# Seven residual stages in split float32: the way up of the feed-forward by feature from the third block on, both parts of x in one 512-column product

## The chip, the core and the metric

The kernel runs on one core of one Trainium2 chip. Its engines are TensorE (PE in the profile; its weight loads are PEld), VectorE (DVE), ScalarE (ACT), GpSimd (POOL) and SyncE (SP), which here issues all DMAs. The metric is the device time of one execution in microseconds; less is better. It includes reading all weights from memory.

## The reference

One sequence of 256 tokens with 1024 features goes through seven residual stages: feed-forward, mLSTM mixer, feed-forward, feed-forward, Mamba-2 mixer, feed-forward, and a hybrid of attention and gated convolution with a final norm. The change touches the four feed-forward stages:

```python
D_FF = ((8 * D_MODEL // 3 + 127) // 128) * 128        # 2816
def swiglu(h, w1, w3, w2):
    return (jax.nn.silu(h @ w1) * (h @ w3)) @ w2

def sublayer(x, fn, g_pre, g_post, shift, scale, gate, weight):
    hmod = rms_norm(x, g_pre) * (1 + scale[:, None, :]) + shift[:, None, :]
    y = rms_norm(fn(hmod), g_post)
    return x + weight * gate[:, None, :] * y
```

Shift, scale and gate of every stage are products of a vector c with a large matrix (the modulation). All data are float32.

## The kernel before

**Arithmetic.** Every large product is made in float32r from split operands: a value is rounded to a high part, and the remainder is the low part. `three` (L1022) issues high x high, high x low and low x high, three matmuls, into the same PSUM region. `xhi` and `xlo` hold the parts of x: features 0 to 1023 in tiles 0 to 7, the gated products of the feed-forward in tiles 8 to 15, always as [feature, token].

**Units.** The weights come in units of 1 MB (128 x 2048). SP loads a unit to a ring of NS = 5 places (`load`, a place is free when its old unit is used), ScalarE rounds it (`hi`, L553), VectorE forms the remainder (`lo`, L1646; in quarters `lo_part`, L1651), and then TensorE may use it (`ready`). `w_in`, `w_hi`, `w_lo` and `w_used` count these steps, each in the order of the units, and every engine has its own place for them in a hand-written order. VectorE also takes two modulation units (`ada`, L1656) per block while they last, nine blocks' worth in a stage (six in the last).

**A feed-forward stage.** The 2816 hidden features are eleven blocks (NF) of 256. The way up of a block takes two units: half 0 has the first 512 input features, half 1 the others, and a unit holds 256 columns of w1 (gate) beside 256 of w3 (up). The way down of a block takes one unit. `first_two` makes blocks 0 and 1 into banks 4 to 7. From the third block on (i = 2 to 10) TensorE runs: the way up by token (`by_token`: x is the stationary operand, the weights are moved, 512 columns; token tile 0 to bank 4, tile 1 to bank 5), and then the way down of block i - 2 (`down`, for two token tiles, into banks 0 to 3, y).

By token the result is [token, feature], and the way down wants [feature, token]. ScalarE takes silu of the gate half (`silu`, L713), VectorE multiplies by the up half (`gate_up`, L1855), TensorE turns the product by four transposes into bank 6 (`turn`, L1238), ScalarE rounds it into `xhi` (`gated_hi`, L717), VectorE forms the remainder into `xlo` (`gated_lo`, L1861). The turn of block i - 1 stands in the middle of block i's way up:

```python
by_token(a, 0, 1, 5).then_inc(w_used, 1)
if i > 2:
    turn(i - 1)
by_token(a + 1, 1, 0, 4).then_inc(s1_ok, 1)
```

**Between stages.** `boundary` stands behind the last block on VectorE and ScalarE: two units of the next stage, the gated y and its mean square (L1743, L618), 1 / rms on GpSimd (L469, L470), the new x (L1750), its mean square, its normed form (L1712), the turn of the new x on TensorE (`turn_x`, L1129), and modulation into `xhi` and `xlo` of the next stage. TensorE meanwhile makes the way down for the second token tile.

**By feature.** The mixers and the last stage have products in another form, `by_feature`: 128 weight columns are the stationary operand, `xhi` or `xlo` (256 tokens) is moved, and the result stands as [feature, token], two feature tiles in a bank.

A bias row for the attention of the last stage is made in the first stage by a small product in bank 7, behind the sixth block, is added on VectorE (L1900) into `wdist`, and goes out to DRAM by a DMA.

## Time and profile before

| | us |
|---|---|
| median of 3 runs | 1431.92 |
| lowest, highest | 1427.91, 1434.92 |
| the profiled execution | 1429.52 |
| span in its profile | 1427.7 |
| TensorE busy | 1397.6 |
| VectorE busy | 1014.4 |
| ScalarE busy | 716.4 |
| GpSimd busy | 90.3 |

Span is from the first to the last instruction of the profiled execution; its time has 1.8 us more around it. In rows of the timeline the bracket at the end says how long the engine idled ahead of the row and for whom. A matmul's duration includes the time in which its results drain, so that following ones overlap: what one costs is the distance of starts. The four stages with the change lie between 51 and 215, 340 and 519, 530 and 708, and 933 and 1108 us, roughly.

### The profile page before, as it was taken

The numbers are of one execution on the slowest core, as the hardware profiler recorded it, in microseconds if no ns is written. First come the engines' busy times: TensorE is split into PE (matmuls) and PEld (weight loads), VectorE is DVE, ScalarE is ACT, GpSimd is POOL, SyncE is SP. The second block draws the span as 40 slices with busy tenths as digits, with TensorE's granted clock in tenths as the row PEclk, the third lists the DMA queues.
The fourth block names the chain that finished last, engine by engine and source line by source line (L and its number), as shares of the span: only waits on it lengthen the run. The fifth ranks groups of instructions, "written<-read, shape, count | busy, mean of one in ns | idle before, by whom it ended". The sixth has DMA issues, their size and how long they took to land.

```text
span 1427.7 us, 18521 instructions
## 1 busy us (share of the span) xinstructions
PE 1397.6 (98%) x7566; PEld 1199.3 (84%) x7566; DVE 1014.4 (71%) x1280; ACT 716.4 (50%) x927; POOL 90.3 (6%) x118
## 2 busy tenths in 40 slices
PE   9999999998999999999999999999999999999997
PEld 8788888887888878888789978788888899999886
DVE  5887677977977768877768976678746634653865
ACT  5543456456533455444565676554335544545433
POOL 1000001002000010000000352100000100000000
PEclk9999999999999999999999999999999999999999
DMA  9898865745987848888535612488755554455542
GB/s 385 353 345 295 325 232 206 311 179 199 392 318 296 317 169 317 317 312 331 199 137 188 210 71 89 177 302 335 288 194 206 184 205 157 148 175 180 193 152 112
DMA packets 50500, 339.10 MB, mean 238 GB/s; under 512 B 6720, under 2 KB 8432, under 8 KB 10352
## 3 DMA queue, kind: packets, MB, share of 16 engines
q1 hardware_dynamic: 50416, 337.92, 63.8%
q8 instruction: 60, 0.98, 0.3%
q14 instruction: 24, 0.20, 0.0%
HBM read 336.81 MB, written 2.66 MB: 238 GB/s over the span
## 4 chain that ended last, share of the span: by engine, by line
PE 79%; DVE 11%; ACT 4%; DMA 3%; issue 2%; POOL 1%; SPq 0%; ACTq 0%; POOLq 0%; DVEq 0%
PE ps L1020 76%; DMA raw<-units 3%; DVE wlo L1646 3%; DVE hf L2068 2%; ACT whi L553 1%; PE ps L1238 1%; DVE M L1656 1%; PE ps L1129 1%; ACT hf L634 1%; POOL ssx L470 0%; POOL base L469 0%; DVE xlo L1721 0%; DVE wlo L1651 0%; DVE unit_at L1646 0%; ACT xhi L638 0%
## 5 line engine op out<-in xcount | busy, mean ns | idle before, releaser
L1646 DVE TENSOR_TENSOR wlo<-raw,whi 128x2048 fp32r<-128x2048 f32 x212 | 486.1, 2298 | 203.4 <-ACT whi L553 203.0
L1020 PE MATMUL ps<-whi,xhi 128*128 128x512 f32 x1432 | 568.1, 397 | 7.0 <-DVE wlo L1651 1.7
L1020 PE MATMUL ps<-whi,xlo 128*128 128x512 f32 x1432 | 558.5, 390 | 0.0
L1020 PE MATMUL ps<-wlo,xhi 128*128 128x512 f32 x1432 | 558.3, 390 | 0.0
L553 ACT ACTIVATE whi<-raw 128x2048 fp32r<-128x2048 f32 x218 | 416.8, 1914 | 159.7 <-DMA raw<-units 159.6
L1020 PEld LDWEIGHTS ps<-whi,xhi 128*128 128x128 f32 x1432 | 269.2, 188 | 68.6 <-issue 4.7
L1020 PEld LDWEIGHTS ps<-whi,xlo 128*128 128x128 f32 x1432 | 269.0, 188 | 57.7
L1020 PEld LDWEIGHTS ps<-wlo,xhi 128*128 128x128 f32 x1432 | 269.5, 188 | 52.5
L1020 PE MATMUL ps<-xhi,whi 128*128 128x256 f32 x704 | 201.9, 287 | 0.1
L1020 PE MATMUL ps<-xlo,whi 128*128 128x256 f32 x704 | 199.1, 283 | 0.0
L1020 PE MATMUL ps<-xhi,wlo 128*128 128x256 f32 x704 | 199.1, 283 | 0.0
L1656 DVE SCALAR_TENSOR_TENSOR M<-M 128x1024 f32<-128x1024 f32 x160 | 189.2, 1219 | 0.1
L1020 PEld LDWEIGHTS ps<-xhi,whi 128*128 128x128 f32 x704 | 135.0, 192 | 0.7 <-ACT hf L824 0.3
L1020 PEld LDWEIGHTS ps<-xlo,whi 128*128 128x128 f32 x704 | 135.0, 192 | 0.3
L1020 PEld LDWEIGHTS ps<-xhi,wlo 128*128 128x128 f32 x704 | 134.9, 192 | 0.0
L717 ACT ACTIVATE xhi<-ps 128x512 fp32r<-128x512 f32 x44 | 26.3, 598 | 133.8 <-PE ps L1238 133.7
L713 ACT ACTIVATE M<-ps 128x256 f32<-128x256 f32 x88 | 33.3, 380 | 91.8 <-PE ps L1020 89.4
L469 POOL TENSOR_SCALAR base<-ssx 128x1 f32<-128x1 f32 x28 | 17.5, 626 | 955.6 <-ACT M L618 617.7
L1855 DVE TENSOR_TENSOR M<-M,ps 128x256 f32<-128x256 f32 x88 | 35.9, 417 | 30.8 <-ACT M L713 30.8
L951 ACT ACTIVATE M<-ps 128x512 f32<-128x512 f32 x28 | 16.7, 597 | 66.0 <-PE ps L1020 65.9
L1861 DVE TENSOR_TENSOR xlo<-ps,xhi 128x512 fp32r<-128x512 f32 x44 | 30.3, 688 | 25.4 <-ACT xhi L717 25.2
L2068 DVE SCALAR_TENSOR_TENSOR hf<-hf,cols 128x253 f32<-128x253 f32 (+2 forms) x72 | 36.8, 552 | 7.8 <-ACT hf L824 6.8
(249 smaller groups left out, 976.9 us busy)
## 6 DMA issues: line engine op xcount, KB each, us to landing
raw<-units SPq DMA_DIRECT2D x218, 1024.0 KB, 4.9
M<-ada_units SPq DMA_DIRECT2D x82, 1024.0 KB, 7.0
M<-units SPq DMA_DIRECT2D x10, 1024.0 KB, 6.3
gp<-gate_rows SPq DMA_DIRECT2D x7, 512.0 KB, 7.6
bias_copies<-bias_by_distance SPq DMA_DIRECT2D x1, 1536.0 KB, 9.4
M<-cvec SPq DMA_DIRECT2D x2, 512.0 KB, 4.4
x<-x_in SPq DMA_DIRECT2D x1, 1024.0 KB, 6.0
ada_a<-ada_units SPq DMA_DIRECT2D x1, 1024.0 KB, 18.8
```

What stands on the lines that cost most here:

```text
L469: step(pool.tensor_scalar(base[:, 0:1], a, b, EPS, ALU.add, ALU.add))
L553: act.activation(rounded(u), landed(u), ACT.Copy).then_inc(w_hi, 1)
L634: r = act.activation(hf[:, k, t_], ps[:, 2 * t + q // 2, (k % 4) * P:(k % 4 + 1) * P], ACT.Identity, scale=g1T[:, n, k:k + 1], bias=shT[:, ...
L713: act.activation(sil[:, t, :], ps[:, bank, 0:FB], ACT.Silu).then_inc(sil_ok[t], 1)
L717: act.activation(xhi[:, 8 + 2 * (i % 4):10 + 2 * (i % 4), :], ps[:, 6, :], ACT.Copy)\
L951: act.activation(hT[:, first + 4 * i + 2 * b:first + 4 * i + 2 * b + 2, :], ps[:, 4 + b, :].rearrange("p (a b) -> p a b", b=SEQ), func)\
L1020: return pe.matmul(out, lhsT, rhs, start=start, stop=stop, skip_group_check=True)
L1646: dve.tensor_tensor(rest(u), landed(u), rounded(u).bitcast(F32), ALU.subtract).then_inc(w_lo, 1)
L1656: return dve.scalar_tensor_tensor(out=w, in0=w, scalar=1.0, in1=cb, op0=ALU.mult, op1=ALU.mult, accum_out=sums[:, column:column + 1])
L1855: dve.tensor_tensor(g[i % 2][:, t, :], sil[:, t, :], ps[:, bank, FB:2 * FB], ALU.mult)\
L1861: dve.tensor_tensor(xlo[:, j:j + 2, :], ps[:, 6, :].rearrange("p (a b) -> p a b", b=SEQ), xhi[:, j:j + 2, :].bitcast(F32), ALU.subtract).t ...
L2068: r = dve.scalar_tensor_tensor(out=cacc[:, q, sh:SEQ], in0=cin[:, q, 0:SEQ - sh], scalar=cols[:, col:col + 1], in1=cacc[:, q, sh:SEQ], op0 ...
```

## The change

From the third block of each feed-forward stage on, the way up is by feature. For each of four feature tiles (two of gate, two of up), 128 weight columns are stationary. The rounded weights are multiplied by `xhi` and `xlo` in one product of 512 columns, for which the two are now views of one tensor `xboth`: the low half of the bank gets high x high, the other half gets the correction high x low. The weights' remainder is multiplied by `xhi` alone, 256 columns, into the low half. The tiles take banks 4 to 7. ScalarE copies the correction out (`correction`), VectorE adds it to the low half (`add_corrections`) into `gate_sum` and `up_sum`, ScalarE takes silu of the gate sum, VectorE multiplies (`product`), ScalarE rounds (`product_hi`), VectorE forms the remainder (`product_lo`). The result is already [feature, token], so turns are left for blocks 0 and 1 alone; they go to banks 0 and 2. `up_free` lets a block's first product wait for the sums of the block before it. In the last block `product_hi` and `product_lo` stand ahead of the rounding and the remainder of the next stage's unit; in the others behind those of the down unit. The product of the bias row moves behind the last block of the first stage, into bank 4, its addition too, and its DMA behind the fifth unit of the mLSTM stage. The gates' semaphores of the two mixers are merged under new names; that part of the diff is left out. Indentation that all lines of a piece have is taken off.

```diff
@@ -93,8 +93,8 @@
 first = -(-nc.sbuf_base // 32) * 32
 raw = sb("raw", [P, NS, UNIT])
 whi = sb("whi", [P, NS, UNIT], F32R)
-xhi = sb("xhi", [P, 16, SEQ], F32R)
-xlo = sb("xlo", [P, 16, SEQ], F32R)
+xboth = sb("xboth", [P, 2, 16, SEQ], F32R)
+xhi, xlo = xboth[:, 0], xboth[:, 1]
 WORDS = 16384
 M = sb("M", [P, WORDS])
 unit_in_M = {at: nc.alloc_sbuf_tensor_at(f"unit_at_{at}", [P, UNIT], F32R,
...
@@ -172,6 +172,7 @@
 negr_sb = m(11536, REL)
 sil = m(12288, T, FB)
 g = [m(12800, T, FB), m(13312, T, FB)]
+gate_sum, up_sum = g
 cb = m(15360, D)
 
 qkT = m(0, 8, SEQ)
...
@@ -368,9 +369,6 @@
     v += 2
 if i == 7:
     gate_out(n)
-    if n == 0:
-        sp.wait_ge(S["wd_ok"], 1)
-        sp.dma_start(scratch[:, :], wdist[0:H_AT, :]).then_inc(S["scratch_out"], 16)
 if i == 9:
     gate_in(n)
     if n == 0:
...
@@ -383,6 +381,9 @@
 for u in range(16):
     if u0 + u not in outside:
         load(u0 + u)
+    if u == 4:
+        sp.wait_ge(S["wd_ok"], 1)
+        sp.dma_start(scratch[:, :], wdist[0:H_AT, :]).then_inc(S["scratch_out"], 16)
     if u == 6:
         sp.wait_ge(w_lo, u0 + 4)
         sp.wait_ge(w_used, u0 + 2)
...
@@ -702,19 +703,31 @@
 for n, kind in enumerate(KIND):
     u0 = FIRST[n]
     if kind == "ffn":
-        b = NF * FFN_NO[n]
+        b, two, nine = NF * FFN_NO[n], 2 * FFN_NO[n], (NF - 2) * FFN_NO[n]
 
         def silu(i, t, bank):
 
-            if b + i:
-                act.wait_ge(g_ok[t], b + i)
+            if two + i:
+                act.wait_ge(g_ok[t], two + i)
             else:
                 act.wait_ge(S["e_used"], EARLY)
             act.activation(sil[:, t, :], ps[:, bank, 0:FB], ACT.Silu).then_inc(sil_ok[t], 1)
 
         def gated_hi(i):
-            act.wait_ge(S["gt_ps"], b + i + 1)
-            act.activation(xhi[:, 8 + 2 * (i % 4):10 + 2 * (i % 4), :], ps[:, 6, :], ACT.Copy)\
+            act.wait_ge(S["gt_ps"], two + i + 1)
+            act.activation(xhi[:, 8 + 2 * i:10 + 2 * i, :], ps[:, 2 * i, :], ACT.Copy)\
+               .then_inc(S["gt_hi"], 1)
+
+        def correction(dst, bank):
+            act.activation(dst, ps[:, bank:bank + 2, SEQ:512], ACT.Copy).then_inc(S["up_corr"], 1)
+
+        def silu_sum(i):
+            act.wait_ge(S["up_sum"], 2 * (nine + i - 2) + 1)
+            act.activation(gate_sum, gate_sum, ACT.Silu).then_inc(S["up_sil"], 1)
+
+        def product_hi(i):
+            act.wait_ge(S["up_g"], nine + i - 1)
+            act.activation(xhi[:, 8 + 2 * (i % 4):10 + 2 * (i % 4), :], up_sum, ACT.Copy)\
                .then_inc(S["gt_hi"], 1)
 
         first_two(n, silu, (lambda: silu_c(1)) if n == 5 else None)
...
@@ -722,14 +735,20 @@
 for i in range(2, NF):
     a = up_unit(n, i, 0)
     hi(a + 3)
-    gated_hi(i - 1)
+    if i == 2:
+        gated_hi(1)
     hi(a + 4)
-    act.wait_ge(s1_ok, (NF - 2) * FFN_NO[n] + i - 1)
-    silu(i, 0, 4)
+    act.wait_ge(s1_ok, nine + i - 1)
+    correction(gate_sum, 4)
     wait_used(act, a + 1)
-    silu(i, 1, 5)
+    act.wait_ge(S["gt_lo"], b + i)
+    correction(up_sum, 6)
+    silu_sum(i)
+    if i == NF - 1:
+        product_hi(i)
     hi(a + 5)
-gated_hi(NF - 1)
+    if i < NF - 1:
+        product_hi(i)
 hi(u0 + 34)
 hi(u0 + 35)
 boundary(n, False)
...
@@ -1226,46 +1245,63 @@
 for n, kind in enumerate(KIND):
     u0 = FIRST[n]
     if kind == "ffn":
-        b = NF * FFN_NO[n]
+        b, two, nine = NF * FFN_NO[n], 2 * FFN_NO[n], (NF - 2) * FFN_NO[n]
 
         def turn(i):
             for t in range(T):
-                pe.wait_ge(g_ok[t], b + i + 1)
-            if b + i:
-                pe.wait_ge(S["gt_lo"], b + i)
+                pe.wait_ge(g_ok[t], two + i + 1)
             for kk in range(2):
                 for t in range(T):
-                    r = pe.transpose(ps[:, 6, kk * SEQ + t * P:kk * SEQ + (t + 1) * P],
-                                     g[i % 2][:, t, kk * P:(kk + 1) * P], ident[:, :])
+                    r = pe.transpose(ps[:, 2 * i, kk * SEQ + t * P:kk * SEQ + (t + 1) * P],
+                                     g[i][:, t, kk * P:(kk + 1) * P], ident[:, :])
             r.then_inc(S["gt_ps"], 1)
+
+        def up_free(i, q):
+
+            if i == 2:
+                pe.wait_ge(g_ok[q // 2], two + q % 2 + 1)
+            elif q % 2 == 0:
+                pe.wait_ge(S["up_sum"], 2 * (nine + i - 3) + q // 2 + 1)
+
+        def up_half(i, half):
+
+            u = up_unit(n, i, half)
+            ready(u)
+            for q in range(4):
+                if half == 0:
+                    up_free(i, q)
+                both = ps[:, 4 + q, :].rearrange("p (a b) -> p a b", b=SEQ)
+                for kk in range(4):
+                    k = 4 * half + kk
+                    w = slice(kk * 512 + q * P, kk * 512 + q * P + P)
+                    mm(both, rounded(u)[:, w], xboth[:, :, k, :], start=(k == 0))
+                    r = mm(ps[:, 4 + q, 0:SEQ], rest(u)[:, w], xhi[:, k, :], stop=(k == 7))
+                if half and q == 1:
+                    r.then_inc(s1_ok, 1)
+            r.then_inc(w_used, 1)
 
         if n:
             first_two(n, before_last=lambda: turn(0))
         else:
             turn(0)
         for i in range(2, NF):
-            a = up_unit(n, i, 0)
-            pe.wait_ge(g_ok[0], b + (i if i > 2 else 1))
-            by_token(a, 0, 0, 4)
-            pe.wait_ge(g_ok[i > 2], b + i)
-            by_token(a, 0, 1, 5).then_inc(w_used, 1)
-            if i > 2:
-                turn(i - 1)
-            by_token(a + 1, 1, 0, 4).then_inc(s1_ok, 1)
+            up_half(i, 0)
             if i == 2:
                 turn(1)
-            by_token(a + 1, 1, 1, 5).then_inc(w_used, 1)
-            if n == 0 and i == 5:
-                pe.wait_ge(S["bias_in"], 48)
-                mm(ps[0:H_AT, 7, 0:REL], rel_sb[0:32, :], oneh_sb[0:32, :], start=True, stop=True)\
-                    .then_inc(S["wd_ps"], 1)
+            up_half(i, 1)
             j = i - 2
             d = down_unit(n, j)
             pe.wait_ge(S["gt_lo"], b + j + 1)
             down(d, 8 + 2 * (j % 4), 0, start=(j == 0))
+            if j == 0:
+                pe.wait_ge(S["gt_lo"], b + 2)
             if i < NF - 1:
                 down(d, 8 + 2 * (j % 4), 1, start=(j == 0)).then_inc(w_used, 1)
-        turn(NF - 1)
+        if n == 0:
+            pe.wait_ge(S["bias_in"], 48)
+            pe.wait_ge(S["up_sum"], 2 * (NF - 3) + 1)
+            mm(ps[0:H_AT, 4, 0:REL], rel_sb[0:32, :], oneh_sb[0:32, :], start=True, stop=True)\
+                .then_inc(S["wd_ps"], 1)
         last = [(down_unit(n, j), 8 + 2 * (j % 4)) for j in range(NF - 3, NF)]
         for j in (1, 2):
             pe.wait_ge(S["gt_lo"], b + NF - 2 + j)
...
@@ -1844,22 +1880,37 @@
 for n, kind in enumerate(KIND):
     u0 = FIRST[n]
     if kind == "ffn":
-        b = NF * FFN_NO[n]
+        b, two, nine = NF * FFN_NO[n], 2 * FFN_NO[n], (NF - 2) * FFN_NO[n]
         v = ADA_FIRST[n]
 
         def gate_up(i, t, bank):
 
-            dve.wait_ge(sil_ok[t], b + i + 1)
-            if t == 0 and i >= 2:
-                dve.wait_ge(S["gt_ps"], b + i - 1)
-            dve.tensor_tensor(g[i % 2][:, t, :], sil[:, t, :], ps[:, bank, FB:2 * FB], ALU.mult)\
+            dve.wait_ge(sil_ok[t], two + i + 1)
+            dve.tensor_tensor(g[i][:, t, :], sil[:, t, :], ps[:, bank, FB:2 * FB], ALU.mult)\
                .then_inc(g_ok[t], 1)
 
         def gated_lo(i):
             dve.wait_ge(S["gt_hi"], b + i + 1)
+            j = 8 + 2 * i
+            dve.tensor_tensor(xlo[:, j:j + 2, :], ps[:, 2 * i, :].rearrange("p (a b) -> p a b", b=SEQ),
+                              xhi[:, j:j + 2, :].bitcast(F32), ALU.subtract).then_inc(S["gt_lo"], 1)
+
+        def add_corrections(i):
+            for j, total in enumerate((gate_sum, up_sum)):
+                dve.wait_ge(S["up_corr"], 2 * (nine + i - 2) + j + 1)
+                dve.tensor_tensor(total, ps[:, 4 + 2 * j:6 + 2 * j, 0:SEQ], total, ALU.add)\
+                   .then_inc(S["up_sum"], 1)
+
+        def product(i):
+            dve.wait_ge(S["up_sum"], 2 * (nine + i - 1))
+            dve.wait_ge(S["up_sil"], nine + i - 1)
+            dve.tensor_tensor(up_sum, gate_sum, up_sum, ALU.mult).then_inc(S["up_g"], 1)
+
+        def product_lo(i):
+            dve.wait_ge(S["gt_hi"], b + i + 1)
             j = 8 + 2 * (i % 4)
-            dve.tensor_tensor(xlo[:, j:j + 2, :], ps[:, 6, :].rearrange("p (a b) -> p a b", b=SEQ),
-                              xhi[:, j:j + 2, :].bitcast(F32), ALU.subtract).then_inc(S["gt_lo"], 1)
+            dve.tensor_tensor(xlo[:, j:j + 2, :], up_sum, xhi[:, j:j + 2, :].bitcast(F32),
+                              ALU.subtract).then_inc(S["gt_lo"], 1)
 
         gate_up(0, 0, 4)
         gate_up(1, 0, 5)
...
@@ -1881,25 +1932,26 @@
     lo(a + 3)
     if some:
         ada(v)
-    gated_lo(i - 1)
-    if i > 2:
-        lo(a + 4)
-    gate_up(i, 0, 4)
-    gate_up(i, 1, 5)
     if i == 2:
-        lo(a + 4)
+        gated_lo(1)
+    lo(a + 4)
+    add_corrections(i)
+    product(i)
+    if i == NF - 1:
+        product_lo(i)
     lo(a + 5)
+    if i < NF - 1:
+        product_lo(i)
     if some:
         ada(v + 1)
         v += 2
     if n == 0 and i == 4:
         ada_done(v - 1)
         gate_columns(0)
-    if n == 0 and i == 5:
-        dve.wait_ge(S["wd_ps"], 1)
-        dve.tensor_tensor(wdist[0:H_AT, :], ps[0:H_AT, 7, 0:REL], negr_sb[0:H_AT, :], ALU.add)\
-           .then_inc(S["wd_ok"], 1)
-gated_lo(NF - 1)
+if n == 0:
+    dve.wait_ge(S["wd_ps"], 1)
+    dve.tensor_tensor(wdist[0:H_AT, :], ps[0:H_AT, 4, 0:REL], negr_sb[0:H_AT, :], ALU.add)\
+       .then_inc(S["wd_ok"], 1)
 ada_done(v - 1)
 for k in {0: (1,), 2: (3,), 3: (4, 5), 5: (6,)}[n]:
     mod_columns(k)

```

TensorE at the start of the third block of the first stage before, behind the turn of block 0 (whi and wlo are a unit's parts; M holds the gated product).

```order
L1020 MATMUL ps<-whi,xlo 128x512
L1238 MATMUL ps<-ident,M 128x128 x4
L1020 MATMUL ps<-whi,xhi 128x512
L1020 MATMUL ps<-wlo,xhi 128x512
L1020 MATMUL ps<-whi,xlo 128x512
```

And the same place now (xboth is both parts of x):

```order
L1039 MATMUL ps<-whi,xboth 128x512
L1255 MATMUL ps<-ident,M 128x128 x4
L1039 MATMUL ps<-xboth,whi 128x512
L1039 MATMUL ps<-xboth,wlo 128x256
L1039 MATMUL ps<-xboth,whi 128x512
```

Three products of 512 columns for one pair of operands became a wide and a narrow one with the weights as stationary operand.

VectorE at the end of the first stage before, from the remainder of the last block's last own units (L1646) to the first unit of the next stage (unit_at):

```order
L1861 TENSOR_TENSOR xlo<-ps,xhi 128x512
L1646 TENSOR_TENSOR wlo<-raw,whi 128x2048
L1855 TENSOR_TENSOR M<-M,ps 128x256 x2
L1646 TENSOR_TENSOR wlo<-raw,whi 128x2048
L1861 TENSOR_TENSOR xlo<-ps,xhi 128x512
L1673 TENSOR_TENSOR shT<-sums,cols 128x8
L1674 TENSOR_TENSOR modc<-sums,cols 128x8
L1675 SCALAR_TENSOR_TENSOR g1T<-modc,cols 128x8
L1685 TENSOR_TENSOR gpc<-sums,cols 128x8
L1686 SCALAR_TENSOR_TENSOR gpc<-gpc,cols 128x8
L1646 TENSOR_TENSOR unit_at_51<-M,unit_at_49 128x2048
L1651 TENSOR_TENSOR wlo<-raw,whi 128x512
```

And now, with L1682 the remainder of a unit, L1901 the sums, L1907 the product, L1912 its remainder and L1953 the bias row:

```order
L1682 TENSOR_TENSOR wlo<-raw,whi 128x2048 x2
L1901 TENSOR_TENSOR M<-ps,M 128x512 x2
L1907 TENSOR_TENSOR M<-M 128x512
L1912 TENSOR_TENSOR xboth<-M,xboth 128x512
L1682 TENSOR_TENSOR wlo<-raw,whi 128x2048
L1953 TENSOR_TENSOR M<-ps,M 8x384
L1709 TENSOR_TENSOR shT<-sums,cols 128x8
L1710 TENSOR_TENSOR modc<-sums,cols 128x8
L1711 SCALAR_TENSOR_TENSOR g1T<-modc,cols 128x8
L1721 TENSOR_TENSOR gpc<-sums,cols 128x8
L1722 SCALAR_TENSOR_TENSOR gpc<-gpc,cols 128x8
L1682 TENSOR_TENSOR unit_at_51<-M,unit_at_49 128x2048
```

The remainder of the next stage's first unit stood ahead of the gate's last step, and stands behind it now, with the bias row after it.

ScalarE at the same place before (L713 silu, L717 rounding of the turned product, L553 rounding of a unit):

```order
L553 ACTIVATE whi<-raw 128x2048
L713 ACTIVATE M<-ps 128x256 x2
L553 ACTIVATE whi<-raw 128x2048
L717 ACTIVATE xhi<-ps 128x512
L553 ACTIVATE unit_at_49<-M 128x2048
L553 ACTIVATE whi<-raw 128x2048
```

And now (L722 the corrections, L726 silu, L730 rounding of the product, L554 rounding of a unit):

```order
L554 ACTIVATE whi<-raw 128x2048 x2
L722 ACTIVATE M<-ps 128x512 x2
L726 ACTIVATE M<-M 128x512
L730 ACTIVATE xboth<-M 128x512
L554 ACTIVATE whi<-raw 128x2048
L554 ACTIVATE unit_at_49<-M 128x2048
L554 ACTIVATE whi<-raw 128x2048
```

The rounding of the next stage's unit moved from in front of the last gate step to behind it.

## Rows read from the trace of the kernel before

**Rows 1.** Busy time by stretch: us, busy time (instructions) by engine, granted clock, DMA.
```profile
568.13:601.76 33.63, 33.63 (x153) 27.82 (x153) 28.01 (x32) 13.81 (x12) 0.00 (x0) 1.00 0.82 316
```

**Rows 2.** Chain of work, two middle blocks: start, us, what.
```profile
568.13 16.38 PE ps L1020 x72
584.51 0.44 PE ps L1238 x4
584.95 16.37 PE ps L1020 x72
```

**Rows 3.** Timeline of TensorE at products by feature: start, us, instruction.
```profile
734.08 0.28 PE L1020 MATMUL ps<-xhi,mbw_two 128*64 128x256 f32 x1
...
735.84 0.28 PE L1020 MATMUL ps<-xlo,mbw_two 128*64 128x256 f32 x1
...
1150.00 0.28 PE L1020 MATMUL ps<-xlo,whi 128*128 128x256 f32 x1
...
1154.68 0.28 PE L1020 MATMUL ps<-xlo,whi 128*128 128x256 f32 x1
...
1309.60 0.40 PE L1020 MATMUL ps<-whi,xhi 128*128 128x512 f32 x1
...
1310.30 0.40 PE L1020 MATMUL ps<-whi,xhi 128*128 128x512 f32 x1
```

**Rows 4.** Groups, 568.13 to 601.76: count, busy us, mean ns, idle before.
```profile
L1646 DVE TENSOR_TENSOR wlo<-raw,whi 128x2048 fp32r<-128x2048 f32 x7 | 16.0, 2291 | 5.7 <-ACT whi L553 5.7
L1656 DVE SCALAR_TENSOR_TENSOR M<-M 128x1024 f32<-128x1024 f32 x10 | 11.8, 1218 | 0.0
...
L1861 DVE TENSOR_TENSOR xlo<-ps,xhi 128x512 fp32r<-128x512 f32 x2 | 1.4, 688 | 0.5 <-ACT xhi L717 0.5
```

**Rows 5.** The page's groups for ScalarE; one line's durations on VectorE (min/median/max).
```profile
L553 ACT ACTIVATE whi<-raw 128x2048 fp32r<-128x2048 f32 x218 | 416.8, 1914 | 159.7 <-DMA raw<-units 159.6
...
L717 ACT ACTIVATE xhi<-ps 128x512 fp32r<-128x512 f32 x44 | 26.3, 598 | 133.8 <-PE ps L1238 133.7
...
L1651 DVE TENSOR_TENSOR wlo<-raw,whi x24: 682/684/689, 207.8 to 1108.5; 128x512 fp32r<-128x512 f32 x24
```

**Rows 6.** Timeline at the start of the first stage's third block.
```profile
50.90 0.63 PE L1238 MATMUL ps<-ident,M 128*128 128x128 f32 x4 [0.34 <-DVE M L1855]
...
56.63 0.42 DVE L1855 TENSOR_TENSOR M<-M,ps 128x256 f32<-128x256 f32 x1
```

**Rows 7.** Timeline at the four stages' ends: ScalarE, VectorE, and TensorE's turn.
```profile
198.92 0.38 ACT L713 ACTIVATE M<-ps 128x256 f32<-128x256 f32 x1 [2.33 <-PE ps L1020]
...
204.86 0.16 DVE L1673 TENSOR_TENSOR shT<-sums,cols 128x8 f32<-128x8 f32 x1
...
502.84 0.38 ACT L713 ACTIVATE M<-ps 128x256 f32<-128x256 f32 x1 [2.33 <-PE ps L1020]
...
508.45 0.15 DVE L1673 TENSOR_TENSOR shT<-sums,cols 128x8 f32<-128x8 f32 x1
...
691.37 0.38 ACT L713 ACTIVATE M<-ps 128x256 f32<-128x256 f32 x1 [2.33 <-PE ps L1020]
...
697.36 0.16 DVE L1673 TENSOR_TENSOR shT<-sums,cols 128x8 f32<-128x8 f32 x1
...
708.31 1.09 PE L1129 MATMUL ps<-ident,M 128*128 128x128 f32 x8 [1.00 <-DVE M L1712]
...
1092.97 0.38 ACT L713 ACTIVATE M<-ps 128x256 f32<-128x256 f32 x1 [2.33 <-PE ps L1020]
...
1098.00 0.15 DVE L1673 TENSOR_TENSOR shT<-sums,cols 128x8 f32<-128x8 f32 x1
```

**Rows 8.** The bias row's addition; SP's queue and VectorE behind the first stage.
```profile
L1900 DVE TENSOR_TENSOR M<-ps,M x1: 541/541/541, 120.6 to 120.6; 8x384 f32<-8x384 f32 x1
...
213.50 19.70 SPq L282 DMA_DIRECT2D raw<-units  x3
...
237.82 0.42 DVE L1916 COPY M<-ps 4x256 f32<-4x256 f32 x1
```

34 lines of the change are left out of this document (17 added, 17 removed).

## The prediction

> **What bounds the kernel now.** I read busy times by stretch first, then the chain of work, then the timeline of single blocks. Over two middle blocks of a feed-forward stage TensorE is busy for all of the 33.63 us, at a granted clock of 1.00, the upper of its two levels, 2.4 GHz [rows 1]. The chain shows what it does there: 72 products of 512 columns in 16.38 us, the four turning transposes in 0.44, then the next 72, with nothing between [rows 2]. The period is 16.82 us, and a product of 512 columns costs 227.5 ns from start to start (16.38 / 72). There are 36 such blocks (the third to eleventh of four stages). ScalarE and VectorE have room inside a block: what they do there costs time only where TensorE waits for it. Two kinds of place matter for that, the start of the first stage [rows 6] and the end of each stage, where the norm of the new x stands between two stages [rows 7].
>
> **Part 1, the products.** Before, the way up of a block is 48 products of 512 columns, 48 x 227.5 ns = 10.92 us. After, it is 32 of 512 and 32 of 256: as many columns, 64 instructions instead of 48. The question is what 256 columns cost. In the last stage, where such products run one behind another, 39 of them take 1154.68 - 1150.00 = 4.68 us, 120.0 ns each: 107 for the columns at full clock and 13 beside them, as 227.5 has 14 beside 213. With stationary operands of 64 columns, half the load, 15 of them take 735.84 - 734.08 = 1.76 us, 117 ns each, so the load of weights is hardly what sets the 120, and it should not be uncovered when wide and narrow alternate [rows 3]. Such an alternation is not in the trace. I take 227.5 + 120 = 347.5 ns for a pair. From below, the 117 gives 344.5. From above, the first three gaps of wide products behind a run of narrow ones take 1310.30 - 1309.60 = 0.70 us, 233 ns each [rows 3]; a pair would be 353. I stay at 347.5, since the two long runs hold every part of a product once, and the 233 follows a single change of form. 32 x 347.5 = 11.12 us: the way up gets **0.20 us slower** a block. The wide product reads two runs of 256 columns, 4096 elements apart, instead of one of 512; no row shows that form, and I cost it at nothing, within the same two bounds.
>
> The Trainium skill, "TensorE: Matmul & The Clock Gate", section "Back-to-back issue gap", gives N / 2.4 + 2.5 ns for an isolated product at full clock. By it the way up would lose, as an estimate, 16 x 2.5 ns = 0.04 us a block instead of 0.20, and the whole would come out 5.8 us better. The trace does not agree: it has 13 to 14 ns where the rule has 2.5 [rows 2, 3].
>
> **Part 2, the turns.** Nine of eleven turns a stage go. Each is 0.44 us of TensorE on the path [rows 2]. Blocks four to eleven each lose the one in the middle of their way up: 8 x (0.44 - 0.20) = 1.92 us a stage, **7.7 us** in four. The third block keeps its turn and pays its 0.20: +0.8 us in four. The turn of the eleventh block lies in the stage's end, part 4.
>
> **Part 3, inside a block.** ScalarE gives up two operations of 256 columns and one of 512 for four of 512, at about 0.60 us each [rows 5], and has idle time. VectorE gives up two products of 0.42 [rows 6] and a subtraction of 0.69 [rows 4] for four operations of about 0.68 [rows 5]. With three remainders of units (2.29 each) and two modulation units (2 x 1.22 each) [rows 4] that makes 14.5 us of VectorE in a block of 16.6. It still fits. The new wait is up_free: the next block's first product needs the gate sum. Between the end of the way up and that wait TensorE has 24 products of the way down, 5.46 us. The correction's copy (0.60) and the sum (0.69) need 1.3 of them, so the cover is some 4 us with VectorE free, and shorter by what VectorE still has to do of the unit's remainder ahead of the sum (2.29). Cost: none. Queued behind the sums are the remainder of a down unit, wanted a block later, and a modulation unit.
>
> At the start of the first stage the cover is missing. The third block begins behind the turn at 50.90, at 51.34, and its fourth feature tile 12 pairs later, at 55.5 us. That tile overwrites bank 7, which is held until VectorE's product that starts at 56.63 and takes 0.42 [rows 6]: TensorE waits **1.5 us**. In the other three stages the first two blocks end later and in another order of banks, and this product is done by then.
>
> The bias row's product stays as long as it was. Its small DMA moves on the sync engine's queue from the first stage into the second, behind that stage's fifth unit, which is the first of the three issued from 213.50 on. VectorE waits for it ahead of the gate rows, whose first copy starts at 237.82 [rows 8]. A landing could take 20 us without being seen: no cost.
>
> **Part 4, the end of a stage.** Let E be the moment at which ScalarE starts on the last block's second half: 198.92, 502.84, 691.37 and 1092.97 [rows 7]. Before, VectorE is through with the unit and the gate, and starts the modulation columns, at 204.86, 508.45, 697.36 and 1098.00 [rows 7], so 5.94, 5.61, 5.99 and 5.03 us after E. From there a row of dependent work leads to the turn of the new x, for which TensorE waits (1.00 us in the third) [rows 7]. After, the order puts the whole gate chain ahead of the next stage's unit: copy of the correction 0.60, sum 0.69, product 0.68, rounding of the product 0.60, rounding of the unit 1.92, its remainder 2.29 [rows 4, 5]. This is 6.78 us; following instructions of one engine overlap by 0.1, hand-overs cost about as much, and I take 6.7. The lags are 0.76, 1.09, 0.71 and 1.67, **4.2 us** in all. In the first stage the addition of the bias row, 0.54 [rows 8], now stands there too: 4.8 us. The turn of 0.44 that goes makes TensorE come earlier to the wait, and buys nothing.
>
> **Sum.** -7.7 + 0.8 + 1.5 + 4.8 = **-0.6 us**. The profiled execution took 1429.52 us, 1427.7 of them span; by the sum it would take 1428.9. The median of the runs shown is 1431.92, 2.4 above it, so I forecast 1431.3 us.
>
> **Rivals.** (a) *A pair costs more than its parts*, 353 ns as behind a run of narrow products. There are 36 x 32 = 1152 pairs, 1.15 us for every ns: +6.3 us, 1437.6. From 354.3 ns on it is slower by over half a per cent. For it: the 233 ns, and the new form of the moving operand. Against: the 117 ns. (b) *The narrow product's fixed part is hidden* behind the wide one, 107 instead of 120: 13.3 ns a pair, -15.3 us, 1416. Against it: no run in the trace comes below 117. The skill's rule above points this way, and gives 1425.5 with its 5.8 us. (c) *The end of a stage isn't delayed*, since the norm waits for something later than VectorE's order: 4.2 us less, 1427.1; with 344.5 ns a pair, 1423.6. (d) *VectorE becomes the bound*, slower than before. With modulation units it has 14.5 us of work in 16.6, and the gate sum stands behind a remainder and a modulation unit. If its copy of the work starts so late that the sum comes after the 5.46 us of the way down, TensorE stands at each of some 30 blocks; 0.5 us each is +15 us, 1446. Against it: in two blocks VectorE idles 5.7 us in front of remainders, waiting for ScalarE [rows 4].
>
> **How the numbers follow.** Chances: the forecast 0.50, (a) 0.17, (b) 0.10, (c) 0.14, (d) 0.09. The forecast's own range is 1427 to 1435. The range that holds eight in ten reaches down to (c) with cheap pairs, 1423, and up past (a) with three more us of waits, 1441. Half a per cent is 7.2 us, about what a measurement of this kernel can tell from no change. Below 1424.8 lie (b) and half of (c): 0.17. Above 1439.1 lie (d) and the upper half of (a): 0.19. Within: 0.64.
>
> **What would show it.** A middle block's period of 16.6 us; starts 227 and 120 ns apart in its way up; one wait of 1.5 us near 55 us, for VectorE's gate product; at each stage's end a wait of 2 to 3 us for the new x instead of up to 1. It is wrong if a pair is off by over 5 ns, if TensorE waits for the gate sum in middle blocks, or if the turn of the new x does not come later after E.

## The result, and the profile after

The changed kernel takes 1441.02 us, the median of 6 runs (1438.51 to 1445.52); the kernel before, run beside it, takes 1431.66 (6 runs, 1427.91 to 1434.92). The ratio is 1.0071, with a 95% interval of 1.0056 to 1.0086: slower by 0.7%, where no change that can be measured was forecast, at 1431.3 us. The span of the profiled execution went from 1427.7 to 1436.7 us.

First the blocks. The busy times of two middle blocks after, the stretch that answers to [rows 1] (engines in the order PE, PEld, DVE, ACT, POOL, then granted clock, DMA share and GB/s):

```profile
569.19:602.77 33.58, 33.58 (x177) 28.61 (x176) 29.98 (x32) 17.34 (x17) 0.00 (x0) 1.00 0.85 327
```

TensorE still has no gap, and two blocks take 33.58 us instead of 33.63. So the turn that each block lost has bought 0.05 us in two blocks. The timeline of TensorE in one of these blocks shows why (start, us, instruction):

```profile
569.19 0.39 PE L1039 MATMUL ps<-xboth,whi 128*128 128x512 f32 x1
...
570.12 0.28 PE L1039 MATMUL ps<-xboth,wlo 128*128 128x256 f32 x1
570.24 0.40 PE L1039 MATMUL ps<-xboth,whi 128*128 128x512 f32 x1
570.48 0.28 PE L1039 MATMUL ps<-xboth,wlo 128*128 128x256 f32 x1
...
580.48 0.40 PE L1039 MATMUL ps<-whi,xboth 128*128 128x512 f32 x1
...
582.81 0.39 PE L1039 MATMUL ps<-wlo,xboth 128*128 128x512 f32 x1
...
585.98 0.39 PE L1039 MATMUL ps<-xboth,whi 128*128 128x512 f32 x1
```

The way up runs from 569.19 to 580.48: 11.29 us for 32 pairs, 352.8 ns each. The forecast had 347.5, that is 11.12 us. From the wide product's start to the narrow one's are 235.9 ns on average in this stage, and 116.9 back. VectorE and ScalarE do what was worked out, and TensorE waits for neither of them in the middle blocks. The groups of VectorE in the same two blocks (count, busy us, mean ns, idle before them), which answer to [rows 4]:

```profile
L1682 DVE TENSOR_TENSOR wlo<-raw,whi 128x2048 fp32r<-128x2048 f32 x7 | 16.0, 2288 | 3.0 <-ACT whi L554 3.0
L1692 DVE SCALAR_TENSOR_TENSOR M<-M 128x1024 f32<-128x1024 f32 x8 | 9.4, 1218 | 0.0
L1901 DVE TENSOR_TENSOR M<-ps,M 128x512 f32<-128x512 f32 x4 | 2.7, 683 | 0.6 <-ACT M L722 0.6
```

Then the start of the first stage. It waits where it was said to, for the product of gate and up (the timeline of TensorE and VectorE, the stretch of [rows 6]):

```profile
57.04 0.41 DVE L1889 TENSOR_TENSOR M<-M,ps 128x256 f32<-128x256 f32 x1
...
57.51 0.50 PE L1039 MATMUL ps<-xboth,whi 128*128 128x512 f32 x1 [1.40 <-DVE M L1889]
```

Last the ends of the stages. First ScalarE and VectorE at the third one, then the turns of the new x at all four, the rows that answer to [rows 7]:

```profile
698.23 0.60 ACT L722 ACTIVATE M<-ps 128x512 f32<-128x512 f32 x1 [2.22 <-PE ps L1039]
...
704.99 0.16 DVE L1709 TENSOR_TENSOR shT<-sums,cols 128x8 f32<-128x8 f32 x1
...
217.13 1.09 PE L1148 MATMUL ps<-ident,M 128*128 128x128 f32 x8 [1.48 <-DVE M L1748]
...
524.62 1.97 PE L1148 MATMUL ps<-ident,M 128*128 128x128 f32 x8 [2.32 <-DVE M L1748]
...
715.96 1.97 PE L1148 MATMUL ps<-ident,M 128*128 128x128 f32 x8 [2.74 <-DVE M L1748]
...
1117.00 1.09 PE L1148 MATMUL ps<-ident,M 128*128 128x128 f32 x8 [1.78 <-DVE M L1748]
```

VectorE reaches the modulation columns 6.76 us behind ScalarE's start on the last block's second half, where 6.7 was forecast, and the waits are there: 1.48, 2.32, 2.74 and 1.78 us. But in two of the four the eight transposes themselves take 1.97 us, which take 1.09 elsewhere. The busy times by stretch show it in the column of the granted clock (the last but two). First the three stretches behind the waits of 2.32 and 2.74 us and behind a wait of 3.30 us in the mLSTM mixer, then those behind 1.48 and 1.78:

```profile
524.00:527.00 3.00, 2.38 (x10) 2.28 (x11) 1.82 (x5) 1.70 (x4) 0.05 (x1) 0.56 0.34 142
715.00:718.00 3.00, 2.04 (x9) 2.05 (x10) 1.48 (x4) 1.72 (x4) 0.38 (x1) 0.58 0.34 142
275.00:278.00 3.00, 2.72 (x9) 2.39 (x10) 3.00 (x2) 1.80 (x3) 0.00 (x0) 0.53 1.02 429
217.00:220.00 3.00, 2.87 (x17) 2.53 (x18) 2.35 (x8) 2.14 (x7) 0.21 (x1) 1.00 0.49 203
1117.00:1120.00 3.00, 3.00 (x17) 2.62 (x18) 2.35 (x8) 2.15 (x7) 0.35 (x1) 1.00 0.31 131
```

A granted clock near 0.5 is the lower of the two levels, 1.2 GHz. The same instructions of the kernel before and after, set beside each other, come 1.09, 0.99 and 1.26 us later behind these three places (of the last, 0.23 is the wait itself, 3.30 us instead of 3.07): 3.3 us, and no step of the forecast had them. In the kernel before the waits for the new x are at most 1.00 us [rows 7], and the clock behind them stays up, as these two stretches of it show:

```profile
519.00:522.00 3.00, 3.00 (x17) 2.62 (x18) 2.35 (x8) 2.15 (x7) 0.34 (x1) 1.00 0.71 298
708.00:711.00 3.00, 2.69 (x16) 2.38 (x17) 2.35 (x8) 2.15 (x7) 0.03 (x1) 1.00 0.70 298
```

### The profile page after: what moved, and what is told of

Its sections match the earlier page's. It is cut to its first block, busy times and chain, and to the rows that moved or that the text cites. A ratio compares the mean times of both kernels' runs of the same rounds, so it can differ in the third digit from the quotient of the medians.

```text
span 1436.7 us, 19354 instructions
## 1 busy us (share of the span) xinstructions
PE 1398.4 (97%) x7998; PEld 1216.8 (85%) x7998; DVE 1055.5 (73%) x1316; ACT 751.5 (52%) x963; POOL 91.5 (6%) x118
## 4 chain that ended last, share of the span: by engine, by line
PE 79%; DVE 10%; ACT 5%; issue 2%; DMA 2%; POOL 1%; SPq 0%; ACTq 0%; POOLq 0%; DVEq 0%
PE ps L1039 78%; DVE wlo L1682 3%; DVE hf L2120 2%; DMA raw<-units 2%; ACT whi L554 1%; DVE M L1692 1%; PE ps L1148 1%; ACT hf L635 1%; POOL ssx L471 0%; POOL base L470 0%; DVE wlo L1687 0%; DVE xboth L1757 0%; DVE x L1786 0%; ACT xboth L639 0%; DVE unit_at L1682 0%
## 5 line engine op out<-in xcount | busy, mean ns | idle before, releaser
L1039 PE MATMUL ps<-xboth,whi 128*128 128x256 f32 (+1 forms) x2560 | 666.1, 336 | 1.5 <-DVE M L1889 1.4
L1682 DVE TENSOR_TENSOR wlo<-raw,whi 128x2048 fp32r<-128x2048 f32 x212 | 486.2, 2297 | 173.4 <-ACT whi L554 173.0
L1039 PE MATMUL ps<-whi,xboth 128*128 128x512 f32 x1712 | 553.8, 394 | 7.3 <-DVE wlo L1687 1.7
L554 ACT ACTIVATE whi<-raw 128x2048 fp32r<-128x2048 f32 x218 | 416.6, 1913 | 210.2 <-DMA raw<-units 210.2
L1039 PE MATMUL ps<-xboth,wlo 128*128 128x256 f32 x1856 | 522.6, 282 | 0.0
L1039 PEld LDWEIGHTS ps<-xboth,whi 128*128 128x128 f32 x2560 | 436.3, 190 | 56.2 <-DVE M L1889 1.7
L1039 PEld LDWEIGHTS ps<-whi,xboth 128*128 128x128 f32 x1712 | 322.5, 188 | 82.4 <-issue 5.0
L1039 PEld LDWEIGHTS ps<-xboth,wlo 128*128 128x128 f32 x1856 | 352.5, 190 | 1.3
L1039 PE MATMUL ps<-wlo,xboth 128*128 128x512 f32 x856 | 334.3, 391 | 0.0
L1039 PEld LDWEIGHTS ps<-wlo,xboth 128*128 128x128 f32 x856 | 161.4, 189 | 30.5
L722 ACT ACTIVATE M<-ps 128x512 f32<-128x512 f32 x72 | 42.8, 596 | 105.7 <-PE ps L1039 102.3
L1901 DVE TENSOR_TENSOR M<-ps,M 128x512 f32<-128x512 f32 x72 | 48.4, 685 | 39.2 <-ACT M L722 39.1
L970 ACT ACTIVATE M<-ps 128x512 f32<-128x512 f32 x28 | 16.7, 597 | 66.0 <-PE ps L1039 65.9
L726 ACT ACTIVATE M<-M 128x512 f32<-128x512 f32 x36 | 22.5, 625 | 20.5 <-DVE M L1901 20.5
```

The costliest lines, as they stand in the source:

```text
L554: act.activation(rounded(u), landed(u), ACT.Copy).then_inc(w_hi, 1)
L722: act.activation(dst, ps[:, bank:bank + 2, SEQ:512], ACT.Copy).then_inc(S["up_corr"], 1)
L726: act.activation(gate_sum, gate_sum, ACT.Silu).then_inc(S["up_sil"], 1)
L1039: return pe.matmul(out, lhsT, rhs, start=start, stop=stop, skip_group_check=True)
L1682: dve.tensor_tensor(rest(u), landed(u), rounded(u).bitcast(F32), ALU.subtract).then_inc(w_lo, 1)
L1901: dve.tensor_tensor(total, ps[:, 4 + 2 * j:6 + 2 * j, 0:SEQ], total, ALU.add)\
```

## The experiments

Two things were to be explained: 5.3 ns in each of 1152 pairs, 6.1 us, and the waits with the clock behind them. T1, T2 and so on in the expectations name the theories that a run is to part. All edits are made to the kernel after. Where a way up is quoted, it is from the first wide product of a middle block to the first product of the way down, alike in the eight such blocks of the third stage, within 0.01 us. (The fourth block of the first two stages differs; in the kernel after it takes 11.36 and 11.39 us.) A run without a ratio is a single execution, and its time is worth less than its timeline.

### Grouping the products

In group16 a half's sixteen wide products run first and its sixteen narrow ones behind them.

```
+                        for q in range(4):
+                            for kk in range(4):
+                                ...
                                 mm(both, rounded(u)[:, w], xboth[:, :, k, :], start=(k == 0))
+                        for q in range(4):
+                            for kk in range(4):
+                                ...
                                 r = mm(ps[:, 4 + q, 0:SEQ], rest(u)[:, w], xhi[:, k, :], stop=(k == 7))
```

> Of each half of a way up, the 16 wide products now come first and the 16 narrow ones behind them; nothing else is changed from the kernel after. The way up of a middle block took 11.29 us in the kernel after, 352.8 ns a pair, where 347.5 was forecast. Theory T1, the alternation of wide and narrow costs it (a change of form at each product): the way up falls to 32 x 347.5 ns = 11.12 us plus four changes of form of some 5 ns, the period from 16.79 to 16.63 us, the whole by 36 x 0.17 = 6 us, to about 1435 us where the kernel after is at 1441. Theory T2, the wide product itself is slower because its moving operand is two runs of 256 columns: the wide products stand 233 ns apart in a row, the way up stays at 11.29 us and the time at 1441.

It took 1435.72 us (ratio to the kernel before 1.0028, interval 1.0014 to 1.0041). TensorE's timeline in a middle block of it:

```profile
583.07 3.79 PE L1039 MATMUL ps<-xboth,whi 128*128 128x512 f32 x16
586.69 2.08 PE L1039 MATMUL ps<-xboth,wlo 128*128 128x256 f32 x16
588.60 3.82 PE L1039 MATMUL ps<-xboth,whi 128*128 128x512 f32 x16
592.26 2.08 PE L1039 MATMUL ps<-xboth,wlo 128*128 128x256 f32 x16
```

Sixteen wide products take 3.62 and 3.66 us (226 and 229 ns each), sixteen narrow ones 1.91 us (119). The way up is 11.10 us and the period 16.57: the two prices of the forecast hold as long as the forms don't alternate. So the two runs of 256 columns that a wide product reads cost nothing (T2 falls), and the alternation costs the 5.3 ns. By the ratios (1.0071 and 1.0028) the whole fell by 6.2 us, by the medians by 5.3, and not by the 7.9 of 36 x 0.22. Two waits grew: in the first stage the fourth feature tile is reached after 12 wide products instead of 12 pairs, and the wait of 1.40 us became 2.81; at the start of the second one TensorE stands 0.76 us instead of 0.44. Less these 1.7 us, the 7.9 are the 6.2 measured.

The single starts of this run show where a change of form is paid. Behind the sixteen narrow products, the first five gaps between wide ones are 228 to 236 ns, and the later ones 227; the wide products that open a way up, behind products of 512 columns, are 227 ns apart from the first. So the cost isn't in the gap at the change itself, it is spread over the next few products, and each of these five gaps lies between two wide products.

one_run takes the wide product's moving operand from one contiguous run.

```
-                                mm(both, rounded(u)[:, w], xboth[:, :, k, :], start=(k == 0))
+                                mm(both, rounded(u)[:, w], xhi[:, k - k % 2:k - k % 2 + 2, :], start=(k == 0))
```

> The wide product of the way up reads one contiguous run of 512 columns (the high parts of two feature tiles) instead of the high part and the correction of one tile, so it multiplies other data: the correction's share of the way up is left out and another tile's high part stands in its place. Order and sizes are those of the kernel after. T1 (alternation): the pair stays at 353 ns, the way up at 11.29 us. T2 (two runs): the pair falls to 347.5 ns, the way up to 11.12 us, the whole by 6 us.

The way up is 11.29 us, the gaps 236.0 and 116.8 ns, as in the kernel after; the one execution took 1441.12 us. T2 falls a second time.

group4 groups by four, within one feature tile: the loop over four contraction tiles runs once for the wide products and once for the narrow ones.

```
                                 mm(both, rounded(u)[:, w], xboth[:, :, k, :], start=(k == 0))
+                            for kk in range(4):
+                                ...
                                 r = mm(ps[:, 4 + q, 0:SEQ], rest(u)[:, w], xhi[:, k, :], stop=(k == 7))
```

> Within each feature tile's half the four wide products come first and the four narrow ones behind them; nothing else is changed from the kernel after. The way up of a middle block goes from 32 turns of form and back (11.29 us) to 8; with 2 it took 11.13 us. If each time there and back costs 5.3 ns over 347.5 (theory T1/T3, it hangs on the alternation alone), the way up is 11.12 + 8 x 0.0053 = 11.16 us and the period 16.66 to 16.67 us. If the gain of the larger groups came from the order in which the banks are filled, the way up stays near 11.29.

The way up is 11.20 us, the period 16.69; the one execution took 1434.87 us. Two rows of it:

```profile
585.00 1.09 PE L1039 MATMUL ps<-xboth,whi 128*128 128x512 f32 x4
585.93 0.64 PE L1039 MATMUL ps<-xboth,wlo 128*128 128x256 f32 x4
586.40 1.09 PE L1039 MATMUL ps<-xboth,whi 128*128 128x512 f32 x4
```

Four wide ones take 0.93 us (232 ns each), four narrow ones 0.47. It lies between, on the side expected, but 0.04 us above the value for a fixed price for each return: over the 11.10 of two groups, eight returns cost 0.10 us and 32 cost 0.19. The price isn't simply proportional to the number of changes.

### Halving the load of weights

half_load gives the wide product a stationary operand of 64 columns.

```
+                                mm(ps[0:64, 4 + q, :].rearrange("p (a b) -> p a b", b=SEQ), rounded(u)[:, w.start:w.start + 64],
+                                   xboth[:, :, k, :], start=(k == 0))
```

> The wide product of the way up has a stationary operand of 64 columns instead of 128: half of the output rows of the high parts are left out. Order and columns that stream are those of the kernel after. A third theory, T3: in the alternation it is the loading of the wide product's weights that isn't covered, since it lies beside a narrow product of 256 columns only. T3 expects the start of narrow to the start of wide to fall, the pair from 352.8 to about 347.5 ns, the way up from 11.29 to 11.12 us. T1 in its narrow sense (the change of form itself) and T2 (two runs) expect 352.8 ns and 11.29 us as before.

TensorE's timeline at the start of a way up in it:

```profile
579.73 0.40 PE L1039 MATMUL ps<-xboth,whi 128*64 128x512 f32 x1
579.97 0.28 PE L1039 MATMUL ps<-xboth,wlo 128*128 128x256 f32 x1
580.08 0.39 PE L1039 MATMUL ps<-xboth,whi 128*64 128x512 f32 x1
```

The pair falls to 341 ns (gaps 227.2 and 113.6) and the way up to 10.91 us, over twice the step that T3 expected and below the forecast's lower bound of 344.5. T3 also said which gap would fall, that from narrow to wide. It fell by 3.3 ns, and the one from wide to narrow by 8.7. narrow_half halves the narrow product's load instead, both_half halves both, and group16_half has the line of half_load above in the loops of group16.

```
-                                r = mm(ps[:, 4 + q, 0:SEQ], rest(u)[:, w], xhi[:, k, :], stop=(k == 7))
+                                r = mm(ps[0:64, 4 + q, 0:SEQ], rest(u)[:, w.start:w.start + 64], xhi[:, k, :], stop=(k == 7))
```

> The narrow product of the way up has a stationary operand of 64 columns instead of 128: half of the rows of the correction by the weights' low part are left out. The wide product is as in the kernel after. With 64 columns in the wide product's load instead, the gap from wide to narrow was 227.2 ns and from narrow to wide 113.6, where the kernel after has 235.6 and 117.2. Theory T3, the wide product's load lies behind a narrow product too short to cover it: here that load is whole, so the pair stays near 352 ns and the way up at 11.27 us or more. Theory T3b, in the alternation any load costs, whichever product it belongs to: the pair falls by several ns, as far as about 341 (way up 10.9 us).

> Both products of the way up have stationary operands of 64 columns: half of the output rows are left out. Alternation and columns that stream are those of the kernel after. A pair took 352.8 ns with whole loads, 340.8 with half the wide product's (12.0 less) and 346.8 with half the narrow product's (6.0 less). If every load in the alternation costs by its length, the two add up to 334.8 ns a pair and a way up of 10.7 us. If a floor is reached (nothing left uncovered), the pair stays near 340 ns, 10.9 us.

> The 16 wide products of a half come first and the 16 narrow ones behind them, and the wide ones have stationary operands of 64 columns instead of 128: half of the output rows of the high parts are left out. Grouped with whole loads, 16 wide took 3.65 us (228 ns each). Theory T3, it is the alternation that uncovers the wide product's load: in a row of wide products the load is covered whatever its size, the 16 take 3.64 us again, the period of a middle block stays at 16.57 us. Theory T4, half a load makes a wide product cheaper anywhere: the 16 take about 3.56 us and the period falls by 0.15 to 0.2 us.

| kernel | order | load of wide, narrow (columns) | way up, us | pair, ns | time, us |
|---|---|---|---|---|---|
| after | alternating | 128, 128 | 11.29 | 352.8 | 1441.02 (6 runs) |
| half_load | alternating | 64, 128 | 10.91 | 340.9 | 1427.51 |
| narrow_half | alternating | 128, 64 | 11.09 | 346.6 | 1430.03 |
| both_half | alternating | 64, 64 | 10.91 | 340.9 | 1424.58 |
| group16 | groups of 16 | 128, 128 | 11.10 | 346.9 | 1435.72 (10 runs) |
| group16_half | groups of 16 | 64, 128 | 11.20 | 350.0 | 1442.57 |

Where the forms alternate, a shorter load of the wide product's weights brings 12 ns a pair; where they are grouped it brings nothing (the way up is even 0.10 us longer). T3 asks for that much: behind a wide product a load has 227 ns to hide in, behind a narrow one 117, and in the alternation the wide product's load is always behind a narrow one. But T3 isn't shown. The gap that it names is not the one that fell most, the five slow gaps of group16 lie between wide products, whose loads have 227 ns, and rows of wide products with half a load are slower (230 ns a gap in group16_half) than with a whole one (227 to 228). The load of the narrow product brings 6 ns too, though it lies beside a wide one, and only while the other load is whole: with both halved the pair stays on the floor of 340.9, so the two don't add. The theory that any load costs by its length, T3b, falls with that. Half a load is also half of the output rows, and no run here parts the two. What is shown is that the alternation of whole products costs the 5.3 ns and that smaller stationary operands take it away; how the engine comes to it stays open.

No run here measures a load by itself (the profile's 190 ns for one include other parts), and the rule explains only a part of the table: 107 ns is all that a narrow product streams in, and 53 leaves room. But a row of narrow products with whole loads has no more room, and in group16 its products stand only 119 to 120 ns apart.

### The order at the end of a stage

end_order puts the next stage's unit back ahead of the last block's rounding (ScalarE) and remainder (VectorE), as in the other blocks.

```
-                        if i == NF - 1:
-                            product_hi(i)
                         hi(a + 5)
-                        if i < NF - 1:
-                            product_hi(i)
+                        product_hi(i)
...
-                        if i == NF - 1:
-                            product_lo(i)
                         lo(a + 5)
-                        if i < NF - 1:
-                            product_lo(i)
+                        product_lo(i)
```

> The last block of each feed-forward stage is ordered as the other blocks: the rounding of the next stage's unit stands ahead of the rounding of the gate product on ScalarE, and its remainder ahead of the gate rows on VectorE. Nothing else is changed from the kernel after. In the kernel after TensorE waits 1.48, 2.32, 2.74 and 1.78 us at the turn of the new x, and behind the two waits over 2.3 us the granted clock is 0.56 to 0.58 for some 3 us (the eight turning transposes take 1.97 us instead of 1.09), which costs 1.09 and 0.99 us beside the waits. Theory E1, the waits are VectorE's and ScalarE's order alone: the gate rows end about 6.15 instead of 6.75 us behind ScalarE's start on the last block's second half, the waits shrink by 0.5 to 0.6 us each (2 us in all), all lie below 2.3 us, and the clock stays at 1.00: 2 us more, together -4 us, 1437. Theory E2, another part ends the waits: no change of them, and 1441.

It took 1433.94 us (1.0015, interval 1.0004 to 1.0026). The same places at the end of the third stage in the timeline, and then the busy times and the clock around the turn:

```profile
693.82 0.60 ACT L722 ACTIVATE M<-ps 128x512 f32<-128x512 f32 x1 [2.22 <-PE ps L1036]
...
699.58 0.16 DVE L1706 TENSOR_TENSOR shT<-sums,cols 128x8 f32<-128x8 f32 x1
...
698.89 0.39 PE L1036 MATMUL ps<-whi,xboth 128*128 128x512 f32 x1
699.72 0.50 PE L1036 MATMUL ps<-whi,xboth 128*128 128x512 f32 x1 [0.44 <-DVE xboth L1909]
700.05 0.40 PE L1036 MATMUL ps<-wlo,xboth 128*128 128x512 f32 x1
...
710.54 1.09 PE L1145 MATMUL ps<-ident,M 128*128 128x128 f32 x8 [0.99 <-DVE M L1745]
```

```profile
710.00:713.00 3.00, 2.46 (x15) 2.19 (x16) 2.35 (x7) 2.15 (x6) 0.00 (x0) 1.00 0.73 306
```

E1 holds, and its size was too small. VectorE is through 5.76 us after ScalarE's start instead of 6.76, since ScalarE now rounds the unit while VectorE adds and multiplies, and VectorE's remainder of 2.29 us starts 1.6 us sooner (693.82 + 2.95 = 696.77, against 698.23 + 4.55 = 702.78). The turn comes 16.72 us behind that start instead of 17.73, so 1.0 us sooner, in the other two that have a wait 0.7 and 1.0. The wait itself shrinks by 1.75 (2.74 to 0.99), because TensorE now waits earlier, for the later remainder of the gate product: 0.44 us in the bracket, 0.7 in the distance of starts (0.83 and 0.33 us from 698.89 on, instead of 0.23 each). So the waits bring 4.0 us: those for the new x come to 2.2 us in all instead of 8.3, and three waits of the new kind cost 0.7 each. The clock stays at 1.00 at these places, another 2.1 us. That makes 6.1 of the 7.1 us by which the median fell (8.0 by the ratios); the rest isn't accounted for. One fall of the clock in the mLSTM mixer costs another microsecond, and this profile has none there, though the edit doesn't touch that wait (3.44 us).

### The clock

fill leaves every wait's end where it is and only lets TensorE work in it.

```
-                             middle=(lambda: turn_x(n + 1, 0)) if j == 2 else None).then_inc(w_used, 1)
+                             middle=(lambda: (keep_clock(7, 7), turn_x(n + 1, 0))) if j == 2 else None).then_inc(w_used, 1)
...
                     def row_max():
+                        keep_clock(1, 12)
                         pe.wait_ge(S["ml_cols"], 1)
```

> Filler products of 128 columns on a constant tile, whose result nobody reads, are put on TensorE into its long waits: 7 of them (some 0.22 us each, 1.5 us) ahead of the first turning of the new x at the end of each feed-forward stage, 12 (2.6 us) ahead of the wait in the middle of the mLSTM mixer. They only take time in which TensorE stood; nothing else is changed from the kernel after. Theory C1, the granted clock falls because TensorE stands for over 2.3 us: with waits of 0.8 to 1.2 us left the clock stays at 1.00 behind all of them, the eight turning transposes take 1.09 us at each place instead of 1.97 at two, and the time falls by 1.09 + 0.99 + 1.26 = 3.3 us, 1441 to about 1437.7. Theory C2, the fall of the clock has another cause (what TensorE did before, or the stage as such): the clock falls at the same three places and the time stays at 1441.

It took 1438.07 us (1.0047, interval 1.003 to 1.0063), 3 us below the kernel after, as C1 has it. The mean granted clock of its ten executions is 0.994 to 0.999, that of the kernel after's six 0.990 to 0.995. The turn at the end of the third stage in the timeline, and then busy times and clock by stretch at the three places:

```profile
714.37 1.09 PE L1148 MATMUL ps<-ident,M 128*128 128x128 f32 x8 [1.16 <-DVE M L1749]
```

```profile
523.00:526.00 3.00, 2.25 (x16) 1.91 (x15) 1.73 (x5) 2.17 (x4) 0.56 (x1) 1.00 0.49 205
...
713.00:716.00 3.00, 1.84 (x13) 1.52 (x13) 1.52 (x4) 2.18 (x4) 0.71 (x2) 1.00 0.49 205
...
274.00:277.00 3.00, 2.52 (x14) 2.12 (x14) 2.91 (x2) 1.92 (x3) 0.00 (x0) 1.00 1.01 426
```

The turn of the new x comes as long after ScalarE's start as in the kernel after, within 0.02 us. One wait is longer in this profile: TensorE stands 1.64 us at 377.77 for VectorE's gate sum, in the fourth block of the second stage, near where the kernel after has its 0.44.

The profiles together give the count. At the ends of the second and third stage, nine kernels have waits of 2.3 to 2.8 us; the clock fell behind 13 of these 18. The five kernels whose waits there are up to 1.2 us (before, end_order, fill and the two combinations below) show no fall behind any of the ten. Behind the mLSTM mixer's wait of 3.0 to 4.0 us it fell in 8 of 11 profiles, and not in the kernel before, end_order and group4, where that wait is 3.07, 3.44 and 3.49. So a wait of that length puts the clock at risk, and doesn't make it fall each time. Nor is it needed: in group16_half the clock fell behind a wait of 1.92 us, at the start of the second stage. The timeline and the stretch behind it:

```profile
368.39 1.78 PE L1039 MATMUL ps<-xboth,whi 128*64 128x512 f32 x4 [1.92 <-DVE M L1894]
```

```profile
368.50:371.50 3.00, 3.00 (x12) 2.38 (x13) 3.00 (x3) 0.44 (x2) 0.00 (x0) 0.52 0.90 350
```

In the kernel before it fell in the Mamba-2 mixer, at 827.7 us, behind five waits of 0.2 to 0.7 us in the 7 us before. By the Trainium skill, "TensorE: Matmul & The Clock Gate", section "Part 1: The HAM clock gate", the gate watches in windows that run freely, so that it would matter where in one a wait falls; the counts here don't speak against that, and no run tests it.

### The start of the first stage

```
-                    ada(v)
+                    if n:
+                        ada(v)
                     gate_up(1, 1, 7)
+                    if n == 0:
+                        ada(v)
```

> In the first feed-forward stage VectorE's products of gate and up in block two stand ahead of its modulation columns instead of behind them; nothing else is changed from the kernel after. Forecast and trace say that the fourth feature tile of the third block waits 1.40 us for that product, at 57.5 us. If that is VectorE's order alone, the wait is gone and the profiled execution 1.4 us shorter; if another part ends it (a transfer, ScalarE), a wait of over 0.7 us stays.

The wait at 57.5 us is gone, and one of the same length stands ten microseconds later, for the remainder of the second block's gate product:

```profile
67.47 0.50 PE L1039 MATMUL ps<-whi,xboth 128*128 128x512 f32 x1 [1.37 <-DVE xboth L1895]
```

The one execution took 1441.54 us. From the turn at 51.08 to the turn of the new x are 165.79 us; in the kernel after, from 51.31, 165.82. Nothing is won. VectorE works without a gap from 56 us to that wait, so it is VectorE's sum of work that bounds this stretch, and the order only chooses where TensorE pays.

### A combination

combined16 puts group16, end_order and start_order together, with the filler in the mLSTM mixer. combined4 is group4, end_order and that filler.

> The kernel after with three edits: 16 wide products, then 16 narrow ones in each half of a way up; the last block of a stage ordered as the others; in the first stage the products of gate and up ahead of the modulation columns. And 12 filler products in the wait of the mLSTM mixer. From 1441: the grouping 36 x 0.22 = -7.9 us, the order of the ends -4 us of waits and -2.1 us of low clock, the mLSTM's clock -1.3 us: 1425.7 us, so 0.4% under the kernel before (ratio 0.996). The edit in the first stage is expected to bring little, since alone it moved its wait of 1.40 to 10 us later (1.37 us). Were the waits at the ends and the grouping to share their gain, 1429 to 1431 (ratio 0.999).

> The kernel after with groups of 4 wide and 4 narrow products, the last block of a stage ordered as the others, and 12 filler products in the wait of the mLSTM mixer. The grouping brings 36 x 0.13 = -4.7 us instead of -7.9, but the wait in the first stage should stay at 1.4 to 2 us: 1441 - 4.7 - 6.1 - 1.3 = 1429 us, ratio 0.998. If the kernel with 16 is no faster than this one, its larger groups cost elsewhere what they bring on TensorE.

combined16 took 1426.04 us, ratio 0.9959 with an interval of 0.9944 to 0.9974: faster than the kernel before by 0.4%, and than the kernel after by 1.1%. Its waits for the new x are short again, those for the gate product at the start of the first two stages are 0.55 and 0.70 us, and the filler has left 0.9 us of the mLSTM mixer's wait (the view of TensorE's waits: us in total, times, longest):

```profile
PE ps L1145 <- DVE M L1750: 3.3, 5, 1.0
...
PE ps L1036 <- DVE M L1891: 1.3, 2, 0.7
...
PE ps L1036 <- issue: 0.9, 1, 0.9
```

combined4 took 1430.28 us (0.999, 0.9979 to 1.0001), which isn't told from the kernel before. So the change brings a small gain once its costs are taken out. The two combinations differ by 4.2 us, 3.2 of them expected from the larger groups; the rest is not parted from the edit at the start of the first stage, which only combined16 has. The mLSTM mixer's wait is in the kernel before too, and that kernel wasn't run with the filler: up to a microsecond of the gain may not belong to the change.

## Why the prediction was wrong

*The pair (part 1).* This is the step that failed. The two parts, 227.5 and 120 ns, were right, as group16 shows; their sum wasn't the price of the alternation. The 5.3 ns that are missing come to 1152 x 5.3 = **6.1 us**. The 233 ns of [rows 3], the start of a wide product behind narrow ones, was read as the end of the range and given to rival (a), with the argument that half the load brought only 117 instead of 120. That argument compared loads within a run of one form, where a shorter load brings nothing (group16_half); in the alternation it brings 12 ns (half_load). And the 233 ns were no single event: they are the first of the several slow gaps that group16 shows behind narrow products, and an alternation begins with a new change of form each time. Rival (a) named the right cost and price, 1437.6 us, with a chance of 0.17. That the new form of the moving operand costs nothing was right.

*The clock.* No part and no rival had it: **3.3 us** at the lower clock behind waits of 2.32, 2.74 and 3.30 us. Part 4 sized the waits well and took each for its own length alone. The mLSTM mixer's wait stands in the kernel before as well, at 3.07 us, without a fall of the clock in that profile.

*The turns (part 2).* Right in kind: one turn a block goes, 0.44 us. With a pair of 352.8 the way up costs 0.37 more than before, so a block gains 0.07 us instead of 0.24. The period shrank by 0.03 only (33.63 to 33.58 in two blocks), since the way down, whose products are unchanged, takes 5.50 us instead of 5.46: **1.4 us** in 36 blocks that no step had. It lies in the first ten products of the way down: in the timeline above they take 2.33 us (580.48 to 582.81), 233 ns each, and the other fourteen 3.17, 226 each. That looks like the pair's cost once more, paid behind the last change of form, though no run was made for it. In group16 and half_load the way down takes 5.47 us and in both_half 5.45; in group16_half, though grouped, 5.50.

*Inside a block (part 3).* Right for the kernel after. TensorE never waits for the gate sum in a middle block of it (fill and group4 do once, 1.64 and 0.65 us, in the fourth block of the second stage, so the room there is small), and the start of the first stage waits 1.40 us where 1.5 was said. The mechanism of rival (d) is there after all in that one place: start_order shows VectorE as the bound for some ten microseconds. One wait was not foreseen, 0.44 us at the third block of the second stage (375.34 us), for the remainder of the second block's gate product.

*The end of a stage (part 4).* Right in size. VectorE is through 6.76 us after ScalarE's start in three stages and 7.23 in the first, with the bias row, where 6.7 and 7.2 were worked out. From that start the turn comes 1.28, 1.14 and 0.79 us later than before in the first three stages (forecast 1.30, 1.09 and 0.71), and 1.46 in the fourth (1.67). Rival (c) fell; so did (b), since the pair came out above the sum of its parts and not below (half_load, with 340.9, shows that below is possible).

*The sum.* The chances had a small slip: (d) and half of (a) make 0.175, not 0.19. The forecast's -0.6, the pairs' 6.1, the way down's 1.4, the clock's 3.3 and the new wait of 0.4 make +10.6 us. The spans differ by 9.0 (the medians by 9.4), and the profile of the kernel before has a fall of the clock of its own, at 828 us in the Mamba-2 mixer, worth 1.6 us, which that of the kernel after lacks; without it the spans would differ by 10.6. Such falls come and go there from one profile to the next, so the last microsecond of this account is worth little.

## What to carry to other kernels

The price of an instruction in a row of its kind isn't its price between others: short and long products were cheaper here grouped than alternated (by 5 to 6 ns a pair, 5.3 us in the medians), and the gaps at a change of form, few as they are, are the rows to trust. Count how many gaps the change slows, since it isn't the first alone. A wait of TensorE of about 2 us or more has to be priced with the clock behind it, here another 1 us each time that it fell; work in the wait, or an order that shortens it, brought both back at the places tried. And when a wait is to be moved away by another order, ask first whether the engine waited for has any idle time there.

## What the runs showed of the hardware

With 64 columns of stationary operand in the wide product, alternating pairs take 340.9 ns, which is less than the same columns in rows of one form (227.5 + 120); with the same halved load in groups of sixteen, the way up gets 0.10 us longer, not shorter. Neither was expected, and neither is explained. A change from narrow to wide products is paid over the products that follow: with whole loads the first five gaps in group16 and the first ten in the way down of the kernel after are 224 to 241 ns, and then 227; with both loads of the way up halved it is the first two (232 and 231 ns in both_half). Of TensorE's clock, waits of 2.3 to 4.0 us were followed by a stretch at the lower level, of some 3 us and in five cases twice that, in 21 of 29 cases at these three places; of waits up to 1.8 us at the ends of the feed-forward stages, none was, though elsewhere it fell behind 1.92 us and behind several short waits in a row.
